# A two-block transformer kernel: the weight buffers' place in a 1 KB row of SBUF moves from 64 to 96 bytes past the activations'

## Chip, cores, metric

One core of one Trainium2 chip. The metric is the device time of one execution of the whole program, in microseconds (us).

## What is computed

Two blocks run one after the other on `x` of 256 tokens x 1024 features, in float32, each of depth 2:

```python
def first_block(x, mem, ...):
    mem_n = rms_norm(mem, mem_norm_g)
    for l in range(DEPTH):
        h = rms_norm(x, pre_mix_g[l])
        mix = parallel_mixer(h, ...)          # LRU, forgetting attention, retention, then @ w_out
        x = x + rms_norm(mix, post_mix_g[l])
        h = rms_norm(x, pre_cross_g[l])
        x = x + rms_norm(memory_cross_attention(h, mem_n, w_cq[l], w_ck[l], w_cv[l], w_co[l]), post_cross_g[l])
        h = rms_norm(x, pre_ffn_g[l])
        x = x + rms_norm(swiglu(h, w_gate[l], w_up[l], w_down[l]), post_ffn_g[l])
    return x

def second_block(x, ...):
    for l in range(DEPTH):
        x = x + 0.5 * swiglu_2(rms_norm_2(x, ffn1_norm[l]), ...)
        # mixer: NSA, stick-breaking and sliding-window attention of h @ w_in[l], gated and summed, then:
        x = x + merged @ w_out[l]
        x = x + 0.5 * swiglu_2(rms_norm_2(x, ffn2_norm[l]), ...)
    return x
```

There are six feed-forward parts (1024 -> 2 x 2816 -> 1024), one in each layer of the first block and two in each of the second. They and the projections are nearly all of the arithmetic.

## The kernel before, in words

**Layout.** Activations are feature-major: 8 tiles (`KT`) of 128 features on the partitions, 256 tokens (`S`) along the free dimension. So one feature tile of `x`, `xn_hi`, `y_hi` and the like is exactly 1,024 bytes of a partition, and it begins at a fixed place in every 1 KB row. The program counts these places from the start of a 32-byte aligned base: the norms' operands `xn_hi`, `xn_lo`, the feed-forward's `hid_hi`, `hid_lo`, the memory's `mem_hi`, `mem_lo`, the mixer's `merged_hi`, `merged_lo` and the attention's `y_hi`, `y_lo` all begin at place 0.

**Weights.** All weights come as one stream of 332 slots (`ORDER`), each 1024 x 256, in two halves of [128, 4 x 256] float32. SyncE loads half m into ring buffer `raw[m % 4]` as soon as `w_lo` of half m - 4 has been made (`sync_program`). ScalarE copies it, rounded, to `w_hi[m % 4]` (`split_hi`, L919). VectorE writes the rest, `raw - w_hi`, to `w_lo[m % 4]` (`split_lo`, L1455). One feature tile of a weight buffer is 256 columns, 1,024 bytes, as well; a product takes 128 of the columns as its stationary operand, so those begin at the buffer's place or 512 bytes further.

**Products.** `products` (L304) makes a float32 product of three fp32r matmuls into one PSUM bank: hi x hi, hi x lo and lo x hi:

```python
for j, (a, b) in enumerate([(lhs[0], rhs[0]), (lhs[0], rhs[1]), (lhs[1], rhs[0])]):
    m = T.matmul(out, a, b, start=first and j == 0, stop=True, skip_group_check=True)
```

Each has a weight load of 128 columns (a row of the engine PEld in the profile) and streams 256 columns. In `slot_T` the weights are stationary and the activations stream; a slot is 2 halves x 2 column tiles x 4 feature tiles x 3 = 48 matmuls. In `slot_rows` it is the other way round: 128 tokens of `xn` or `mem` are stationary and the weights stream (in the trace, `bank<-w_hi,xn_hi`). A feed-forward part (`ffn`) is 11 gate slots and 11 up slots on `xn`, then 11 down slots on `hid`, 33 x 48 = 1,584 matmuls with hardly a wait between them. Between the parts `keep_busy` (L312) runs bf16 matmuls of 256 columns on `ones` while a norm is made.

**One place with other strides.** In the second block the compression of keys and values (`cmp_hidden_of`) keeps its activations in `y_hi` and `y_lo` as sixteen tiles of 30 columns, one behind the other, so 120 bytes apart, and takes them as stationary operands while the weights stream from the ring: `bank<-w_hi,y_hi 128*30`. Slot `k0` takes the first eight tiles, slot `k1` the last eight. Against the place where the weights' stream begins, the eight tiles of `k1` begin (modulo 1,024) at -128, -8, 112, 232, 352, 472, 592 and 712 bytes.

**Order.** Each engine's instructions are written out by hand, and semaphores join them. In the feed-forward part ScalarE and VectorE split one slot ahead of TensorE.

**The lines that are changed** stand in `build`, where SBUF is handed out in order of the calls:

```python
    x = sb("x", [P, KT, S])
    xn = sb("xn", [P, KT, S])
    xn_hi, xn_lo = sb("xn_hi", [P, KT, S], F32R), sb("xn_lo", [P, KT, S], F32R)
    y_hi, y_lo = sb("y_hi", [P, KT, S], F32R), sb("y_lo", [P, KT, S], F32R)

    sb("offset", [P, 16])
    raw = [sb(f"raw{r}", [P, HK, COLS]) for r in range(RING)]
```

`offset` is 64 bytes that nothing uses. All that is handed out behind it (`raw`, `w_hi`, `w_lo`, `sq`, `con` and the smaller tensors) lies 64 bytes further in the row than it would without it. `hid`, `mem` and `merged` lie ahead of `x`, in a region of their own that begins at the base.

Of the kernel before, what the change touches and what calls it, by code (L numbers as in the profile page):

```python
# [15 lines left out]
P = 128  # L16
# [83 lines left out]
def build(nc, A):  # L100
# [4 lines left out]
    def sb(name, shape, dt=F32):  # L105
        return nc.alloc_sbuf_tensor(name, shape, dt)[tuple(slice(None) for _ in shape)]
# [20 lines left out]
    x = sb("x", [P, KT, S])  # L127
    xn = sb("xn", [P, KT, S])
    xn_hi, xn_lo = sb("xn_hi", [P, KT, S], F32R), sb("xn_lo", [P, KT, S], F32R)
    y_hi, y_lo = sb("y_hi", [P, KT, S], F32R), sb("y_lo", [P, KT, S], F32R)  # L130

    sb("offset", [P, 16])
    raw = [sb(f"raw{r}", [P, HK, COLS]) for r in range(RING)]
    w_hi = [sb(f"w_hi{r}", [P, HK, COLS], F32R) for r in range(RING)]
    w_lo = [sb(f"w_lo{r}", [P, HK, COLS], F32R) for r in range(RING)]
# [2205 lines left out]
def program(nc, arrays):  # L2341
    A = {n: nc.dram_tensor("in_" + n, a.shape, mybir.dt.from_np(a.dtype), kind="ExternalInput").ap()
         for n, a in arrays.items()}
    for n in ("x", "mem"):
        A[n] = A[n].rearrange("p (k s) -> p k s", k=KT)
    A["out"] = nc.dram_tensor("out", (P, KT, S), F32, kind="ExternalOutput").ap()
    A["skew"] = nc.dram_tensor("skew", (P * 12 * VEC,), F32, kind="Internal").ap()
    A["vec"] = nc.dram_tensor("vec", (12, VEC), F32, kind="Internal").ap()
    build(nc, A)
# [12 lines left out]
```

## Time and profile before

| what | us |
|---|---|
| median of 3 runs (lowest to highest) | 2198.8 (2196.2 to 2199.8) |
| the profiled execution's own time | 2195.4 |
| its span, first to last instruction | 2194.1 |
| TensorE busy | 2117.1 (96%) |
| VectorE busy | 1402.8 (64%) |
| ScalarE busy | 1124.8 (51%) |
| GpSimd busy | 72.8 (3%) |
| HBM traffic | 164 GB/s over the span |

The page gives busy times, 40 slices of the span, the DMA queues and the chain of waits that ended last. Matmuls are pipelined: a matmul's row shows how long it lasted, and several overlap, so the rate at which they follow each other is read from their starts, or from the time of a long unbroken piece of the chain divided by the number of matmuls in it.

### The profile page before, as it was taken

To read this page: it belongs to the slowest core of one execution; us is meant where nothing else is said; L and a number is where in the kernel's file an instruction comes from. 1 tells how busy PE (TensorE), PEld (TensorE's weight loads), DVE (VectorE), ACT (ScalarE), POOL (GpSimd) and SP (SyncE) were. 2 spreads that over 40 slices of the span, in tenths; PEclk is the share of its full clock that TensorE was granted. 3 is DMA by queue.
4 is the path that set the end of the run, shared out by engine and by line. 5 is a ranking of instruction groups with operands and counts; after the bars stand their busy time and mean duration, and the time that the engine had idled before them with its cause. 6 is when DMAs were issued, how large, how long until landed. Compare 5 with 4: busy or idle time off the path is not lost.

```text
span 2194.1 us, 40831 instructions
## 1 busy us (share of the span) xinstructions
PE 2117.1 (96%) x17446; PEld 2034.0 (93%) x17446; DVE 1402.8 (64%) x2152; ACT 1124.8 (51%) x1757; POOL 72.8 (3%) x80
## 2 busy tenths in 40 slices
PE   6999999999998999999999999999999999999999
PEld 6889899989888999999997889999999988889999
DVE  5677466565766666566667667666666676677664
ACT  4565444444754544454456556544444466555443
POOL 5100000000000000000000000000000000000000
PEclk9999999999999999999999999999999999999999
DMA  6444346636343456656555324566566553235664
GB/s 221 154 131 142 118 156 201 215 120 198 118 142 98 148 193 203 191 169 196 196 170 173 97 97 153 184 194 206 175 195 208 174 175 125 86 126 177 197 197 150
DMA packets 98485, 360.33 MB, mean 164 GB/s; under 512 B 11136, under 2 KB 11149, under 8 KB 97920
## 3 DMA queue, kind: packets, MB, share of 16 engines
q1 hardware_dynamic: 96192, 349.22, 48.8%
q0 software_dynamic: 1680, 5.35, 0.8%
q8 instruction: 137, 2.24, 0.4%
q10 hardware_dynamic: 432, 3.15, 0.4%
q14 instruction: 44, 0.36, 0.1%
HBM read 356.61 MB, written 3.43 MB: 164 GB/s over the span
## 4 chain that ended last, share of the span: by engine, by line
PE 79%; DVE 13%; ACT 6%; issue 2%; DMA 1%; ACTq 0%; DVEq 0%; SPq 0%
PE bank L304 70%; DVE w_lo L1455 4%; ACT w_hi L919 2%; PE bank L416 1%; DVE rinv L1854 1%; PE bank L330 1%; PE bank L421 1%; DVE xn_lo L1477 1%; DVE sq L1517 1%; DVE x L1521 1%; ACT logit L1330 1%; PE bank L771 1%; PE bank L417 1%; DVE sq L2041 1%; DMA raw<-in_stream 1%
## 5 line engine op out<-in xcount | busy, mean ns | idle before, releaser
L1455 DVE TENSOR_TENSOR w_lo<-raw,w_hi 128x1024 fp32r<-128x1024 f32 x664 | 794.4, 1233 | 380.9 <-ACT w_hi L919 380.4
L304 PE MATMUL bank<-xn_hi,w_hi 128*128 128x256 f32 x3168 | 892.7, 282 | 39.6 <-DVE xn_lo L1477 29.1
L304 PE MATMUL bank<-xn_lo,w_hi 128*128 128x256 f32 x3168 | 881.5, 278 | 0.0
L304 PE MATMUL bank<-xn_hi,w_lo 128*128 128x256 f32 x3168 | 881.4, 278 | 0.0
L919 ACT ACTIVATE w_hi<-raw 128x1024 fp32r<-128x1024 f32 x664 | 672.5, 1050 | 235.7 <-PE bank L304 219.3
L304 PEld LDWEIGHTS bank<-xn_hi,w_hi 128*128 128x128 f32 x3168 | 598.5, 189 | 52.5 <-issue 27.9
L304 PEld LDWEIGHTS bank<-xn_lo,w_hi 128*128 128x128 f32 x3168 | 597.0, 188 | 1.3 <-issue 1.0
L304 PEld LDWEIGHTS bank<-xn_hi,w_lo 128*128 128x128 f32 x3168 | 596.8, 188 | 0.0
L304 PE MATMUL bank<-hid_hi,w_hi 128*128 128x256 f32 x1056 | 292.8, 277 | 0.0
L304 PE MATMUL bank<-hid_hi,w_lo 128*128 128x256 f32 x1056 | 292.8, 277 | 0.0
L304 PE MATMUL bank<-hid_lo,w_hi 128*128 128x256 f32 x1056 | 292.7, 277 | 0.0
L304 PEld LDWEIGHTS bank<-hid_hi,w_hi 128*128 128x128 f32 x1056 | 199.1, 189 | 0.0
L304 PEld LDWEIGHTS bank<-hid_hi,w_lo 128*128 128x128 f32 x1056 | 198.3, 188 | 0.0
L304 PEld LDWEIGHTS bank<-hid_lo,w_hi 128*128 128x128 f32 x1056 | 198.3, 188 | 0.0
L980 ACT ACTIVATE hid_hi<-act_t 128x512 fp32r<-128x512 f32 x66 | 41.7, 632 | 188.8 <-DVE act_t L1535 188.8
L976 ACT ACTIVATE act_t<-act_t 128x512 f32<-128x512 f32 x66 | 41.8, 633 | 180.7 <-DVE act_t L1530 180.7
L304 PE MATMUL bank<-y_hi,w_hi 128*128 128x256 f32 x384 | 108.5, 282 | 3.5 <-DVE y_lo L1465 2.8
L304 PE MATMUL bank<-y_hi,w_lo 128*128 128x256 f32 x384 | 107.0, 279 | 0.0
L304 PE MATMUL bank<-y_lo,w_hi 128*128 128x256 f32 x384 | 107.0, 279 | 0.0
L1465 DVE TENSOR_TENSOR hid_lo<-act_t,hid_hi 128x512 fp32r<-128x512 f32 x66 | 45.7, 693 | 51.0 <-ACT hid_hi L980 51.0
L304 PEld LDWEIGHTS bank<-y_hi,w_hi 128*128 128x128 f32 x384 | 72.3, 188 | 5.7 <-DVE y_lo L1465 3.6
L1535 DVE TENSOR_TENSOR act_t<-act_t,bank 128x512 f32<-128x512 f32 x66 | 45.4, 688 | 46.4 <-PE bank L304 46.4
(373 smaller groups left out, 2706.6 us busy)
## 6 DMA issues: line engine op xcount, KB each, us to landing
raw<-in_stream SPq DMA_DIRECT2D x664, 512.0 KB, 4.2
skew<-vec POOLq DMA_DIRECT2D x12, 192.0 KB, 4.1
table<-skew POOLq DMA_DIRECT2D x1, 1408.0 KB, 7.3
con<-in_con ACTq DMA_DIRECT2D x1, 1029.0 KB, 15.3
x<-in_x ACTq DMA_DIRECT2D x1, 1024.0 KB, 7.0
xn<-in_mem ACTq DMA_DIRECT2D x1, 1024.0 KB, 11.9
out<-x SPq DMA_DIRECT2D x4, 256.0 KB, 3.4
logit<-in_small POOLq DMA_DIRECT2D x3, 288.5 KB, 3.2
```

The source lines that it names most:

```text
L304: m = T.matmul(out, a, b, start=first and j == 0, stop=True, skip_group_check=True)
L330: m = T.matmul(misc[0][:, 0, :], avg, sq[:, k, :], start=k == 0, stop=k == KT - 1, skip_group_check=True)
L416: T.matmul(out, v_of(0), pT[:, 0:S], start=first, stop=False, skip_group_check=True)
L417: return T.matmul(out[:, P:S], v_of(1), pT[:, S:S + P], start=False, stop=last, skip_group_check=True)
L421: m = T.transpose(dst[:, to * P:(to + 1) * P], src[:, frm:frm + P], c("ident"))
L771: T.matmul(out[:, LATE], q[:, P:S], k, start=True, stop=True)
L919: AC.activation(w_hi[m % RING], raw[m % RING], ACT.Copy).then_inc(*hi_done.next())
L976: AC.activation(act_t, act_t, ACT.Silu).then_inc(*silu_made.next())
L980: AC.activation(hid_hi[:, 2 * j:2 * j + 2, :], act_t, ACT.Copy).then_inc(*hid_hi_made.next())
L1455: V.tensor_tensor(w_lo[m % RING], raw[m % RING], w_hi[m % RING].bitcast(F32), ALU.subtract).then_inc(*lo_done.next())
L1465: V.tensor_tensor(lo, src, hi.bitcast(F32), ALU.subtract).then_inc(*to.next())
L1535: V.tensor_tensor(act_t, act_t, dense[1], ALU.mult).then_inc(*up_read.next())
```

## The change

Another unused tensor of 64 bytes goes in ahead of `y_hi`, and the one ahead of the rings shrinks from 64 to 32 bytes. So `y_hi` and `y_lo` begin at place 64, and `raw`, `w_hi`, `w_lo` and all that follows at place 96. The weights are now 96 bytes further in a row than `xn`, `hid`, `mem` and `merged`, and 32 further than `y`. In all 32 bytes more are used. The instructions of every engine, their order and their waits are the same as before; only addresses differ.

```diff
     x = sb("x", [P, KT, S])
     xn = sb("xn", [P, KT, S])
     xn_hi, xn_lo = sb("xn_hi", [P, KT, S], F32R), sb("xn_lo", [P, KT, S], F32R)
+    sb("offset_y", [P, 16])
     y_hi, y_lo = sb("y_hi", [P, KT, S], F32R), sb("y_lo", [P, KT, S], F32R)
 
-    sb("offset", [P, 16])
+    sb("offset", [P, 8])
     raw = [sb(f"raw{r}", [P, HK, COLS]) for r in range(RING)]
     w_hi = [sb(f"w_hi{r}", [P, HK, COLS], F32R) for r in range(RING)]
     w_lo = [sb(f"w_lo{r}", [P, HK, COLS], F32R) for r in range(RING)]
```

## Rows read from the trace of the kernel before

**Rows 1.** The page, busy time by engine, and granted TensorE clock in 40 slices.

```profile
PE 2117.1 (96%) x17446; PEld 2034.0 (93%) x17446; DVE 1402.8 (64%) x2152; ACT 1124.8 (51%) x1757; POOL 72.8 (3%) x80
...
PEclk9999999999999999999999999999999999999999
```

**Rows 2.** The page, the chain that ended last: shares of the span by engine and line.

```profile
PE 79%; DVE 13%; ACT 6%; issue 2%; DMA 1%; ACTq 0%; DVEq 0%; SPq 0%
PE bank L304 70%; DVE w_lo L1455 4%; ACT w_hi L919 2%; PE bank L416 1%; DVE rinv L1854 1%; PE bank L330 1%; PE bank L421 1%; DVE xn_lo L1477 1%; DVE sq L1517 1%; DVE x L1521 1%; ACT logit L1330 1%; PE bank L771 1%; PE bank L417 1%; DVE sq L2041 1%; DMA raw<-in_stream 1%
```

**Rows 3.** Groups by line and form, TensorE: count, busy us, mean ns, idle before.

```profile
L304 PE MATMUL bank<-xn_lo,w_hi 128*128 128x256 f32 x3168 | 881.5, 278 | 0.0
...
L304 PE MATMUL bank<-hid_lo,w_hi 128*128 128x256 f32 x1056 | 292.7, 277 | 0.0
...
L304 PE MATMUL bank<-y_lo,w_hi 128*128 128x256 f32 x384 | 107.0, 279 | 0.0
...
L304 PE MATMUL bank<-w_hi,xn_lo 128*128 128x256 f32 x160 | 46.1, 288 | 0.0
...
L304 PE MATMUL bank<-merged_lo,w_hi 128*128 128x256 f32 x128 | 36.0, 281 | 0.0
L304 PE MATMUL bank<-mem_lo,w_hi 128*128 128x256 f32 x128 | 35.8, 280 | 0.0
...
L304 PE MATMUL bank<-w_hi,mem_lo 128*128 128x256 f32 x128 | 35.7, 279 | 0.0
```

**Rows 4.** The chain in order of time, long pieces: start us, us, what.

```profile
294.06 175.53 PE bank L304 x1488
...
753.90 168.94 PE bank L304 x1488
946.83 174.38 PE bank L304 x1536
...
1393.48 174.37 PE bank L304 x1536
1574.66 174.37 PE bank L304 x1536
...
2021.37 168.94 PE bank L304 x1488
```

**Rows 5.** Groups of VectorE in two stretches, 294 to 464 and 754 to 923.

```profile
L1455 DVE TENSOR_TENSOR w_lo<-raw,w_hi 128x1024 fp32r<-128x1024 f32 x63 | 75.1, 1223 | 45.8 <-ACT w_hi L919 45.8
...
L1455 DVE TENSOR_TENSOR w_lo<-raw,w_hi 128x1024 fp32r<-128x1024 f32 x63 | 75.1, 1223 | 43.7 <-ACT w_hi L919 43.7
```

**Rows 6.** Timeline of TensorE, 469 to 476: start us, us, what (merged).

```profile
471.24 4.97 PE L312 MATMUL bank<-ones 128*128 128x256 bf16 x44
```

**Rows 7.** Timeline of TensorE, slot `k1`: 1st, 19th, 24th product, and what follows.

```profile
1162.27 0.28 PE L304 MATMUL bank<-w_hi,y_hi 128*30 128x256 f32 x1
...
1164.37 0.28 PE L304 MATMUL bank<-w_hi,y_hi 128*30 128x256 f32 x1
...
1164.93 0.28 PE L304 MATMUL bank<-w_hi,y_lo 128*30 128x256 f32 x1
1165.05 0.59 PE L656 MATMUL bank<-sq,con 128*128 128x512 f32 x1
```

**Rows 8.** The page's costliest groups, the weights' split on VectorE.

```profile
L1455 DVE TENSOR_TENSOR w_lo<-raw,w_hi 128x1024 fp32r<-128x1024 f32 x664 | 794.4, 1233 | 380.9 <-ACT w_hi L919 380.4
```

**Rows 9.** Waits: who for whom, us in total, times, longest us.

```profile
PE bank L304 <- DVE w_lo L1455: 15.6, 22, 1.7
ACT w_hi L919 <- DMA raw<-in_stream: 14.2, 10, 3.0
...
SPq L2167 <- DVE w_lo L1455: 1941.0, 660, 24.6
```

**Rows 10.** The page's DMA issues: KB each, median us from issue to landing.

```profile
raw<-in_stream SPq DMA_DIRECT2D x664, 512.0 KB, 4.2
```

## The prediction

> **What bounds the kernel now.** I read the page's busy times first. TensorE works in 96% of the span, at full clock in every slice [rows 1]. VectorE, the next, has 64%. Then the chain that ended last: 79% of it lies on TensorE, 70% on one line, L304, the fp32r products. 13% lies on VectorE: 4% is the split of the weights (L1455), and the rest is norms and attention [rows 2]. So the kernel is a stream of some 15,700 products of 256 columns (from the counts in [rows 3] and their equals), and its time is this count by the pace of one.
>
> The pace is what must be read next, since the change touches no instruction. A row of matmuls shows latency (277 to 281 ns), not pace, because they overlap. The pace is in the chain's long pieces, where time over count gives it [rows 4]. The kernel has six feed-forward blocks of 33 slots x 48 = 1,584 products. Five of them show 168.94 / 1488 = 113.5 ns (twice), and 174.38 / 1536 = 113.5 ns (three times). The first block shows 175.53 / 1488 = 118.0 ns. The tiles, lines and shapes are the same, and the clock is full in both. The reader is to see that **the stream has two paces**, 113.5 and 118.0 ns. It keeps the one that it starts with for up to 175 us, and the difference is (175.53 - 168.94) / 1488 = 4.43 ns per product.
>
> VectorE is not the cause: its weight split takes 1223 ns in the slow block and 1223 ns in a fast one [rows 5]. The bf16 matmuls of the same 256 columns, which keep TensorE busy between blocks, run at (4.97 - 0.28) / 43 = 109.1 ns [rows 6], so both paces lie above what the engine can do with this many columns.
>
> **How much runs at the slow pace** can be read from mean durations. The products on `merged` last 36.0 / 128 = 281.3 ns, those on `hid` 292.7 / 1056 = 277.2 ns. One `hid` block in six is slow, so the fast duration is 277.2 - (281.3 - 277.2) / 5 = 276.4 ns. On this scale `xn` (278.2) is 38% slow, `y` (278.6) 46%, `mem` 67% (279.7) where it streams and 51% (278.9) where the weights do [rows 3]. The products with `xn` stationary (288.1) I count as slow altogether, though waits lengthen them too. That makes 3,600 + 530 + 530 (hid) + 380 (merged) + 260 + 200 + 480, about 6,000 products, and 6,000 x 4.43 ns = 26.5 us spent on the slow pace. It is an upper figure, because a product behind a wait is long as well. I take 24 us.
>
> **The change, part by part.**
>
> *Instructions.* Each queue issues the same instructions in the same order on the same tiles; none is added or removed, and no wait. That is 0 us.
>
> *The distance between the two operands of a product.* Before, weights lie 64 bytes further in a 1 KB row than `xn`, `hid`, `mem`, `merged` and `y`. Now it is 96 bytes for all but `y`, and 32 for `y`. A product streams one operand's 1,024 bytes while the next one's 512 bytes (128 columns) are loaded. Does distance act on the pace? Two readings of the trace point in different ways. Against: the weights' distance is +64 or -64 by which operand streams, and 512 more for the second column tile, and `mem`, `xn` and `y` show no third pace: the pieces are at 113.5 or 118. For: the compression's products [rows 7] take stationary tiles of 30 columns, each 120 bytes further than the last, against a stream that always begins at the same place. The first six tiles (18 products) take (1164.37 - 1162.27) / 18 = 117 ns each. The last two come at (1164.93 - 1164.37) / 5 = 112 ns. They begin 592 and 712 bytes past the stream's own start. So somewhere in the row the slow pace cannot hold, and the place of the load does matter. A shift of 32 bytes is a quarter of one such step, and 96 is still far from 592. So I take no new pace, and the share of the slow one as it is: **0 us**. The bounds come from the same rows: all products at 113.5 is -24 us, all at 118.0 is 9,700 x 4.43 ns = +43 us.
>
> The Trainium skill ("SBUF — State Buffer", section "SBUF: two separate sides") says that only the port pair shared by VectorE and GpSimd causes contention, and that TensorE never waits on anyone there. It also gives cachelines of 16 bytes, of which 32 is a multiple. By that page the layout could cost or bring nothing, and the sum would be 0 us. This trace agrees that VectorE is out of it [rows 5], but two paces for the same products [rows 4] are something the page does not foresee.
>
> The Trainium skill ("TensorE: Matmul & The Clock Gate", "Back-to-back issue gap") gives N / 2.4 + 2.5 ns, which is 109.2 ns for 256 columns. The bf16 row agrees with 109.1 ns [rows 6]; the fp32r products, at 113.5, do not.
>
> *Splits, norms, attention.* `raw`, `w_hi` and `w_lo` move together, so the split reads and writes at the same distances as before. Its mean over stages of different neighbours moves from 1223 [rows 5] to 1233 ns [rows 8], 0.8%. Taken on the 4% of the chain that it holds (88 us) this is 0.7 us either way, and I take 0. `sq`, the constants and the score buffers move by 32 bytes too; the same 0.8% on the other 9% of VectorE's share is 1.6 us.
>
> *The weights' transfers.* 512 KB land 4.2 us after issue, and SyncE waits for VectorE to free a buffer in 660 of 664 cases, 1941 us in total [rows 9, 10]; TensorE waited 15.6 us for weights, ScalarE 14.2 us for a transfer. A landing slower by a few tenths of a microsecond at an odd 32 bytes would be covered by this slack: 0 us, and at most the doubling of the 14.2 us.
>
> The sum is 0 us. The profiled execution took 2195.4 us (span 2194.1), 3.4 under the median of 2198.8, and the runs shown span 3.6 us. I predict against the median: 2198.8 us. A measurement of this kernel can tell about 0.2%, 4.4 us, from no change.
>
> **The rivals.**
>
> 1. *The slow pace goes, or mostly does.* At 96 bytes the load may no longer meet what holds it. For it: near 592 bytes it does not hold, and 96 is a step in that direction (608 for the second column tile, already past it). Against: at 64 and 576 it holds. All gone gives 2175; only the first feed-forward block turned fast gives 1,584 x 4.43 = -7 us, 2192. Chance 0.34, partial cases included.
>
> 2. *More blocks start slow* (the other side). A block keeps the pace of its first products, so the start decides, and one slow start costs 7.0 us. The price is at the head of a feed-forward block, on TensorE; it decides from one further block on: 2206 for one, 2220 for three. For it: the first block shows that such a start happens, and the compression's tiles at 112 bytes and beyond are slow [rows 7], to which 96 is nearer than 64. Against: five of six start fast. Chance 0.16.
>
> 3. *The fast pace is lost altogether*: +43 us, 2242. For it: `merged` never has the fast one [rows 3]. Against: `hid` at the same distance has it. Chance 0.14.
>
> 4. *The pace falls to the bf16 one*, 109.1 ns: 9,700 x 4.4 + 6,000 x 8.9 = 96 us, 2103. Nothing in the rows shows an fp32r product stream there. Chance 0.03.
>
> 5. *The change does nothing*, because only whole rows or 64-byte pieces count, or since the paces come from timing alone. It gives my forecast, and is part of its chance.
>
> **How the numbers follow.** My forecast (shares of both paces within about 1,000 products of now, 2194 to 2203) has 0.33. Faster by over 0.2% has rivals 1 and 4: 0.37. Slower has rivals 2 and 3: 0.30. The range goes from 2172, all of rival 1 with 3 us of scatter, to 2225, rival 2 with three blocks and the scatter. It leaves out rivals 3 and 4, 0.17. The likeliest case's own range is 2194 to 2203.
>
> **What would show it.** Right: the chain's six long pieces again at 113.5 or 118.0 ns, one slow; `hid` near 277 ns; the split at 1233 ns; landing at 4.2 us. Rival 1: `hid`, `xn` and `merged` near 276 ns. Rivals 2 and 3: `hid` at 278 or more, 281 if all is lost. A third pace, in any long piece, would prove the step wrong in which the distance is given no new pace; a changed split or landing, those on the splits and the transfers.

## The result and the profile after

The changed kernel takes 2240.0 us (median of 4 runs, 2238.3 to 2244.6) against 2199.1 us (4 runs, 2196.2 to 2199.8): the ratio is 1.0172, with a 95% interval of 1.0129 to 1.0214. It is slower by 41 us, outside the range of 2172 to 2225. The profiled execution took 2238.3 us, span 2237.0.

The page's busy times, clock, and chain, as in [rows 1, 2]:

```profile
span 2237.0 us, 40831 instructions
...
PE 2166.3 (97%) x17446; PEld 2083.6 (93%) x17446; DVE 1403.0 (63%) x2152; ACT 1125.6 (50%) x1757; POOL 72.8 (3%) x80
...
PEclk9999999999999999999999999999999999999999
...
PE 82%; DVE 11%; ACT 5%; issue 1%; DMA 0%; DVEq 0%; ACTq 0%; SPq 0%
```

The counts are the same and the clock is full in every slice. TensorE is busy 49.2 us longer, VectorE 0.2 us and ScalarE 0.8 us. The loss is on TensorE alone. The chain's long pieces (start us, us, what), the six feed-forward blocks, answer to [rows 4]:

```profile
295.77 174.86 PE bank L305 x1488
...
757.33 174.86 PE bank L305 x1488
956.24 180.49 PE bank L305 x1536
...
1410.78 180.49 PE bank L305 x1536
1598.09 182.54 PE bank L305 x1536
...
2056.31 176.86 PE bank L305 x1488
```

Time over count gives 117.5 ns per product in four blocks and 118.9 or 118.8 ns in two (called 118.8 below). Counted from the start of one product to the start of the next, every level is about 0.2 ns lower (117.3 here, 113.3 and 117.8 before), since a piece's time also holds a little of its first and last product. **The pace of 113.5 ns is gone, and the levels are others**: before, a block ran at 113.5 or at 118.0. The six pieces hold the same 9,072 products as before and take 1070.1 us instead of 1036.5, which is 33.6 us of the 42.9 us by which the span grew. Outside the blocks the fast pace is gone too: no 25 products in a row with loads of 128 columns start less than 117.2 ns apart on average, where before the least was 113.3 ns.

The groups by line and form, against [rows 3]:

```profile
L305 PE MATMUL bank<-xn_lo,w_hi 128*128 128x256 f32 x3168 | 889.5, 281 | 0.0
L305 PE MATMUL bank<-hid_lo,w_hi 128*128 128x256 f32 x1056 | 295.9, 280 | 0.0
...
L305 PE MATMUL bank<-y_lo,w_hi 128*128 128x256 f32 x384 | 107.9, 281 | 0.0
L305 PE MATMUL bank<-w_hi,xn_lo 128*128 128x256 f32 x160 | 46.6, 291 | 0.0
...
L305 PE MATMUL bank<-merged_lo,w_hi 128*128 128x256 f32 x128 | 35.9, 280 | 0.0
```

`hid` went from 277.2 to 280.2 ns, `xn` from 278.2 to 280.8, `y` from 278.6 to 281.0. `merged`, all of whose products were slow in the profiled execution of before, lost nothing (281.3 to 280.5).

What the forecast held for unchanged is unchanged. The split on VectorE and the transfers, against [rows 8, 10]:

```profile
L1456 DVE TENSOR_TENSOR w_lo<-raw,w_hi 128x1024 fp32r<-128x1024 f32 x664 | 794.5, 1232 | 391.4 <-ACT w_hi L920 390.9
...
raw<-in_stream SPq DMA_DIRECT2D x664, 512.0 KB, 4.2
```

And the waits, against [rows 9], where TensorE's wait for weights fell by 4.1 us. A slower stream leaves the engines that feed it more time, which would explain it; no run tests that.

```profile
PE bank L305 <- DVE w_lo L1456: 11.5, 20, 1.5
```

### The profile page after: what moved, and what is told of

It reads as the page before. It is cut to its first block, busy times and chain, and to the rows that moved or that the text cites. A ratio compares the mean times of both kernels' runs of the same rounds, so it can differ in the third digit from the quotient of the medians.

```text
span 2237.0 us, 40831 instructions
## 1 busy us (share of the span) xinstructions
PE 2166.3 (97%) x17446; PEld 2083.6 (93%) x17446; DVE 1403.0 (63%) x2152; ACT 1125.6 (50%) x1757; POOL 72.8 (3%) x80
## 4 chain that ended last, share of the span: by engine, by line
PE 82%; DVE 11%; ACT 5%; issue 1%; DMA 0%; DVEq 0%; ACTq 0%; SPq 0%
PE bank L305 73%; DVE w_lo L1456 3%; PE bank L417 1%; ACT w_hi L920 1%; DVE rinv L1855 1%; PE bank L422 1%; PE bank L331 1%; PE bank L772 1%; DVE xn_lo L1478 1%; PE bank L418 1%; DVE sq L1518 1%; DVE x L1522 1%; DVE sq L2042 1%; DMA raw<-in_stream 0%; DVE scale L1496 0%
## 5 line engine op out<-in xcount | busy, mean ns | idle before, releaser
L1456 DVE TENSOR_TENSOR w_lo<-raw,w_hi 128x1024 fp32r<-128x1024 f32 x664 | 794.5, 1232 | 391.4 <-ACT w_hi L920 390.9
L1531 DVE TENSOR_TENSOR act_t<-bank,scale 128x512 f32<-128x512 f32 x66 | 45.6, 691 | 53.3 <-PE bank L305 53.1
```

The lines of the kernel that those rows point to most:

```text
L1456: V.tensor_tensor(w_lo[m % RING], raw[m % RING], w_hi[m % RING].bitcast(F32), ALU.subtract).then_inc(*lo_done.next())
L1531: V.tensor_tensor(act_t, dense[0], scale_2, ALU.mult).then_inc(*gate_read.next())
```

## The experiments

Every experiment is the kernel before with other places in the row. "Distance" is how far the rings lie past `xn`, `hid`, `mem` and `merged`, in bytes (`y` too, unless said). Where a diff shows only the line of `offset`, its width gives the distance: `[P, 16]` is 64.

### Is it the distance, the place, or something else that moved?

**128 bytes for all.**

```diff
-    sb("offset", [P, 16])
+    sb("offset", [P, 32])
```

> Weights 128 bytes further in the 1 KB row than all activations (64 before, 96 in the change). Theory A, the pace depends on the distance between the two operands modulo 64 bytes (0 allows 113.5 ns per product, 32 does not): 128 is 0 modulo 64, so about 2199 us, within 10 us, and feed-forward pieces of the chain at 113.5 or 118.0 ns. Theory B, it is the absolute place of the weights, off a 64-byte boundary: 128 is on one, so also about 2199 us. Theory C, the distance itself, the larger the worse: 2240 us or more, and no long piece at 113.5 ns.

Measured: 2250.1 us against 2199.2, ratio 1.0214 (1.0133 to 1.0296). The first feed-forward piece:

```profile
296.10 176.84 PE bank L304 x1488
```

That is 118.8 ns. Theory A falls, and theory B, since the rings are back on a multiple of 64 bytes from the base here, as before.

**Everything by 32 bytes, distance 64.**

```diff
+    sb("shift", [P, 8])
     base = (nc.sbuf_base + 31) // 32 * 32
```

> Every tensor of the kernel before moved by 32 bytes, activations and weights together, so the distance stays 64 and only the absolute places go off the 64-byte boundaries. Theory A (distance modulo 64): about 2199 us, within 10 us, long pieces at 113.5 or 118.0 ns. Theory B (absolute place of the weights): about 2240 us, long pieces at 117.3 to 120 ns as in the changed kernel. Theory C (size of the distance): about 2199 us.

Measured: 2201.6 us (8 runs) against 2199.2, ratio 1.0005 (0.9974 to 1.0036). Two blocks of the chain:

```profile
1585.78 174.37 PE bank L305 x1536
2032.87 168.95 PE bank L305 x1488
```

113.5 ns again, with every tensor 32 bytes off the places of before. So this shift of the absolute places costs nothing; what the two operands have between them does. Other common shifts were not run.

**Only what lies behind the rings, by 32 bytes.**

```diff
+    sb("offset_rest", [P, 8])
     sq = sb("sq", [P, KT, S])
```

> Rings and y stay where they were before; only what lies behind the rings (squares, constants, small operands, score buffers) moves by 32 bytes, as in the change. Theory D, the loss comes from norms and attention through these tensors: a good part of the 41 us, above 2215 us. Theories A, B and C: within 5 us of before, 2194 to 2204 us.

Measured: 2199.4 us (8 runs) against 2199.2, ratio 0.9997 (0.9958 to 1.0036). Theory D falls: norms, constants and score buffers have no part in it.

**Only `y`, by 32 bytes (distance 32 for `y`, 64 for the rest).**

```diff
+    sb("offset_y", [P, 8])
     y_hi, y_lo = sb("y_hi", [P, KT, S], F32R), sb("y_lo", [P, KT, S], F32R)
...
-    sb("offset", [P, 16])
+    sb("offset", [P, 8])
```

> Only y_hi and y_lo move, by 32 bytes; rings, constants and all else stay at their places of before, so the distance is 32 for the attention outputs' streams and 64 for the rest. Theory: the change's loss lies in each stream by its own distance. The y streams (1,152 products) go to 118.5 ns, at most 5 ns x 620 products that were at 113.5, so +3 us; xn and hid keep 113.5 or 118.0 ns, and the time is that of before on this chip within 8 us.

Measured: 2199.5 us (8 runs) against 2203.6 (21 runs), ratio 0.9987 (0.9957 to 1.0017). Groups by form:

```profile
L305 PE MATMUL bank<-xn_lo,w_hi 128*128 128x256 f32 x3168 | 880.1, 278 | 0.0
L305 PE MATMUL bank<-hid_lo,w_hi 128*128 128x256 f32 x1056 | 292.3, 277 | 0.0
...
L305 PE MATMUL bank<-y_lo,w_hi 128*128 128x256 f32 x384 | 107.9, 281 | 0.0
```

`y` has the 281 ns of the changed kernel, `xn` and `hid` keep the 278 and 277 of before. Each stream follows its own distance. The half of the change that moves `y` costs less than this measurement tells. By subtraction, the loss lies in the 96 bytes of the rest.

**TensorE's own reads, or the other engines?** When the rings move, so does all that ScalarE, VectorE and the transfers read and write in them. These accesses could slow the stream instead of TensorE's own. The kept traces can settle this. Every stretch of six products in a block was sorted by what another engine did in it: idle means busy for under 5% of the stretch, busy over 95%. The mean time from one start to the next, in ns, is:

| block | VectorE idle / busy | ScalarE idle / busy | no DMA packet in flight / some all the time |
|---|---|---|---|
| before, first (slow) | 117.77 / 117.79 | 117.78 / 117.78 | 117.80 / 117.78 |
| before, second (fast) | 113.31 / 113.35 | 113.35 / 113.33 | 113.36 / 113.33 |
| changed, first | 117.33 / 117.33 | 117.33 / 117.33 | 117.33 / 117.33 |

The levels are the same whatever the others do, so no access of theirs at that moment makes them. What is left is TensorE's load of one operand and its stream of the other.

### Which distances have the fast pace?

**32 bytes.**

```diff
-    sb("offset", [P, 16])
+    sb("offset", [P, 8])
```

> Weights only 32 bytes further than all activations, y included. Theory A (modulo 64) and theory B (absolute place): about 2240 us, all long pieces at 117.3 ns or above. Theory C (the larger the distance the worse): faster than 2199 us or the same, with long pieces at 113.5 ns.

Measured: 2249.8 us, ratio 1.0213 (1.0127 to 1.0299), and 118.5 ns in every block:

```profile
296.00 176.34 PE bank L304 x1488
```

Theory C falls with it: a smaller distance is as bad as a larger one.

**192 bytes** (`[P, 48]`).

> Weights 192 bytes further than all activations. So far 64 gave 2199 us, and 32, 96 and 128 gave 2240 to 2250. Theory E, the pace depends on the distance modulo 128 bytes and only near 64 can a stream run at 113.5 ns: 192 is 64 modulo 128, so about 2199 us within 12, with xn and hid pieces at 113.5 or 118.0 ns. Theory C (the further, the worse, past 64): 2240 us or more. Theory F, the period is longer than 128 (256, 512 or the whole row): 2240 us or more too.

Measured: 2240.0 us against 2214.1, ratio 1.0118 (1.0064 to 1.0171). Feed-forward blocks all ran at 118.0 ns, so the time that theory E gave, that of before within 12 us, did not come. But 113.5 ns exists here too. In this stream, in which the weights stream past stationary `xn`, the 44 products from the first row to the second take 4.99 us, 113.4 ns each (timeline of TensorE: start us, us, what):

```profile
82.85 0.28 PE L304 MATMUL bank<-w_hi,xn_hi 128*128 128x256 f32 x1
...
87.84 0.28 PE L304 MATMUL bank<-w_hi,xn_lo 128*128 128x256 f32 x1
```

So 192 has the levels of 64, and more of its streams start in the slow one.

**No offset** (the line of `offset` removed).

> No offset: weights and activations begin at the same place of a row. Theory E (modulo 128): 0 is the same as 128, so about 2250 us, with long pieces at 118.5 or 120 ns. If the period is longer than 128 the levels differ from those of 128 bytes: any other pace.

Measured: 2267.7 us, ratio 1.0242 (1.0213 to 1.0272), with 120.2 ns in every block:

```profile
298.60 178.81 PE bank L303 x1488
```

At 128 bytes five blocks had 118.8, the last 120.2. So 0 and 128 share one level, and whether they share both is not shown by one profiled execution of each.

**576, 448 and 320 bytes** (`[P, 144]`, `[P, 112]`, `[P, 80]`).

> Weights 576 bytes further: 64 plus 512, so the two column tiles of a weight buffer (512 bytes apart) change places, and the set of distances, 64 and 576 modulo the row, is the one of before. Theory H, only these distances modulo 512 count: pieces at 113.5 or 118.0 ns alone, time within 15 us of before on this chip. If the size of the distance counted: all at 117 ns or above, 40 us more.

> Weights 448 bytes further, which is 64 short of 512: the mirror of 64 if only distances modulo 512 count. The streams of before in which the weights stream and xn is stationary had this distance and showed 113.5 and 118.0 ns. Expected: the same two levels for all streams, the share of 113.5 open (192 had the levels too, but little of the fast one). If the sign counts: no piece at 113.5.

> Weights 320 bytes further, 64 modulo 128 and 256. If the levels repeat every 128 bytes: pieces at 113.5 or 118.0 ns only, as at 64 and at 192, time between before and 2245 us. If the period is longer: other levels, such as 118.5 or 120.

Measured against 2203.6 us: 2201.8 for 576 (ratio 1.0006, 0.9960 to 1.0052), 2233.2 for 448 (1.0162, 1.0082 to 1.0243), 2210.6 for 320 (1.0020, 0.9975 to 1.0064). One block at 118.0 ns and one at 113.5 from the chain of each, in this order:

```profile
1584.36 181.18 PE bank L304 x1536
2038.42 168.94 PE bank L304 x1488
```

```profile
1599.24 181.18 PE bank L304 x1536
2055.08 168.92 PE bank L304 x1488
```

```profile
752.14 175.52 PE bank L304 x1488
951.70 174.37 PE bank L304 x1536
```

The blocks of all three have the two levels of 64 and no other. So the fast level comes back at every distance tried that is 64 modulo 128, and at no other. In the one profiled execution of each, two of six blocks were fast at 576, one at 448 and four at 320.

**How many streams are fast sets the time.** In the profiled execution of each kernel that has the two levels, each unbroken run of 24 or more products with the same activations was counted as fast or slow by its mean pace (the line drawn at about 115 ns):

| kernel | slow products | us | us less 4.43 ns for each |
|---|---|---|---|
| before | 4,805 | 2195.4 | 2174.1 |
| only `y` moved | 4,745 | 2196.6 | 2175.5 |
| only the rest moved | 4,089 | 2198.9 | 2180.7 |
| all moved | 7,122 | 2206.9 | 2175.4 |
| 320 | 5,668 | 2208.4 | 2183.3 |
| 576 | 8,418 | 2212.5 | 2175.2 |
| 448 | 12,154 | 2229.1 | 2175.3 |
| 192 | 14,054 | 2235.1 | 2172.9 |

The times spread over 40 us. With the slow products taken off at the price of the prediction, six of the eight agree within 2.6 us, though they come from several chips; two have 5 to 10 us more, which stay unexplained. So 192 and 448 lose their time because few of their streams are fast, and not by another pace.

### How wide is the place around 64?

**80 and 48 bytes.** The rings are given places with `sb_at` inside one block, since `sb` rounds to 32 bytes; for 80:

```diff
-    sb("offset", [P, 16])
-    raw = [sb(f"raw{r}", [P, HK, COLS]) for r in range(RING)]
...
+    ring_at = (nc.sbuf_base + 31) // 32 * 32 + 64
+    sb("rings", [P, 12 * HK * COLS + 24])
+    ring = lambda name, dt, n: sb_at(name, [P, HK * COLS + 8], dt, ring_at + 4096 * n)[
+        :, 4:4 + HK * COLS].rearrange("p (k c) -> p k c", k=HK)
+    raw = [ring(f"raw{r}", F32, r) for r in range(RING)]
...
```

> Weights 80 bytes further, 16 past the place of before. It asks how wide the good place is. Theory E with a place some 32 bytes wide (as the compression's tiles of 30 columns suggest, of which 72 and 80 bytes modulo 128 ran at 113.5): 2175 to 2210 us, pieces at 113.5 ns. If only the exact 64 is good: 2235 us or more, no piece at 113.5 ns.

> Weights 48 bytes further, 16 short of the place of before. Theory E with a place centred on 64: like 80 bytes, 2175 to 2210 us. With a place that begins at 64 and lies above it: 2235 us or more, and 80 is the better of the two.

Measured against 2214.1 us: 2265.7 for 80 (ratio 1.0234, 1.0182 to 1.0285), 2242.2 for 48 (1.0128, 1.0085 to 1.0170). No block is at 113.5 in either: 80 has 119.0 ns in five and 118.8 in one, 48 has 118.0 in all. A fast place some 32 bytes wide, by which both were expected at 2175 to 2210 us, falls.

**56, 72, 60 and 68 bytes**, with the same lines and other numbers:

> Weights 56 bytes further, 8 short of 64. At 64 a stream can run at 113.5 ns or at 118.0 by its start; at 48 and 80 only at 117.5 or more. If the good place has a width of 8 bytes or more to this side: pieces at 113.5 ns, time at or below before. If the fast pace here holds from any start: all six long pieces at 113.5 ns and about 24 us less than before on this chip. If not: 118 ns throughout and 2235 us or more.

> Weights 72 bytes further, 8 past 64. Same question to the other side: with a width of 8 bytes pieces at 113.5 ns, and if any start leads there about 24 us less than before on this chip; without it 118 ns or more throughout and 2240 us or more.

> Weights 60 bytes further, one float32 element short of 64. With a good place at least one element wide to this side: both levels or the fast one alone, at most the time of before. If the place is exactly 64 modulo 128: no piece at 113.5 ns, 2235 us or more.

> Weights 68 bytes further, one element past 64. As for 60, to the other side: both levels or the fast one alone if the place is wider than one element, otherwise no piece at 113.5 ns and 2235 us or more.

Measured against 2202.4 us: 2242.8 for 56 (ratio 1.0192, 1.0116 to 1.0267), 2246.4 for 72 (1.0208, 1.0151 to 1.0265), 2261.4 for 60 (1.0276, 1.0217 to 1.0335), 2249.0 for 68 (1.0220, 1.0158 to 1.0281). The first block of 60 and of 68 in the chain:

```profile
297.47 178.06 PE bank L307 x1488
```

```profile
295.81 176.35 PE bank L307 x1488
```

119.7 and 118.5 ns. One float32 element to either side of 64 and the fast pace is gone from all six blocks.

Two things besides the distance set these six kernels apart. Their weights begin off a multiple of 32 bytes, which no kernel with the fast pace has, and their rings are handed out by `sb_at`, which was not run at 64 itself. The split on VectorE keeps its 1232 to 1234 ns and the transfers their 4.1 to 4.2 us in all six, but whether TensorE's fast pace needs the distance or an aligned place as well is not separated. What is shown is that, of the places tried, only those 64 bytes apart modulo 128, all multiples of 32, have it.

| distance | ns per product in the six blocks | time / before |
|---|---|---|
| 0 | 120.2 | 1.0242 |
| 32 | 118.5 | 1.0213 |
| 48 | 118.0 | 1.0128 |
| 56 | 118.0 | 1.0192 |
| 60 | 119.7 | 1.0276 |
| 64 | 113.5 or 118.0 | 1 |
| 68, 72 | 118.5 | 1.0220, 1.0208 |
| 80 | 118.8 or 119.0 | 1.0234 |
| 96 (the change) | 117.5 or 118.8 | 1.0172 |
| 128 | 118.8 or 120.2 | 1.0214 |
| 192 | 118.0 (113.5 in short streams) | 1.0118 |
| 320, 448, 576 | 113.5 or 118.0 | 1.0020, 1.0162, 1.0006 |

The ratios come from several chips, each measured against its own runs of the kernel before. They rest on two runs of each changed place, but on four for 96 and eight for 320 and 576. None of these places beats 64 by more than its interval.

## Why the prediction was wrong

**The reading was right.** TensorE's stream bounds the kernel, its time is count by pace, and the pace has levels that a block keeps from its start. The instructions, the split (1233 to 1232 ns), the transfers (4.2 us before and after) and the rest behind the rings (ratio 0.9997 by itself) cost nothing, as each was priced. Two readings were a little off. I took some 6,000 slow products and 24 us; the count, in runs of 24 or more, is 4,805 and 21 us. And the compression's last two tiles do not run at 112 ns: from the 19th product to what follows the 24th, (1165.05 - 1164.37) / 6 is 113.3 ns [rows 7], which is the fast pace and no other.

**The step that failed** is the one on the distance: "So I take no new pace, and the share of the slow one as it is: 0 us." In its place stands: at 96 and at 32 bytes no block and no long stream ran at 113.5 ns, and the blocks have 117.5, 118.5 or 118.8 ns. The argument against an effect was that distances of +64, -64 and 512 more all show the same two paces. That holds, and it was read the wrong way. All of these are 64 modulo 128, the one class that has the fast pace, so they could not show what another class does. The trace of before had no product of `products` with loads of 128 columns outside that class.

**The bound was right where the choice was not.** Rival 3, the fast pace lost altogether, gave 2242 us; 2240.0 was measured. I gave it a chance of 0.14 and left it out of the range. Its price was 9,700 products by 4.43 ns, from 113.5 to 118.0. That it fits so well is in part luck, since the blocks have lost the level of 118.0 ns as well; they happen to average 1070.1 us / 9,072 = 118.0 ns. Measured by blocks, the five that were fast lost 4.0 or 5.3 ns a product (113.5 to 117.5 or 118.8), and the first, which had been slow, won 0.45 ns (118.0 to 117.5). The argument against it, that `hid` keeps the fast pace at the same distance as `merged`, spoke of 64 bytes and not of 96.

**The compression's tiles misled.** I took from their last two [rows 7] that the fast place lies near 592 and 712 bytes and is some width apart from 64. In the changed kernel the good tiles of the same slot are others (1st, 10th, 19th and 24th product):

```profile
1177.93 0.28 PE L305 MATMUL bank<-w_hi,y_hi 128*30 128x256 f32 x1
...
1178.98 0.28 PE L305 MATMUL bank<-w_hi,y_hi 128*30 128x256 f32 x1
...
1180.01 0.28 PE L305 MATMUL bank<-w_hi,y_hi 128*30 128x256 f32 x1
...
1180.60 0.28 PE L305 MATMUL bank<-w_hi,y_lo 128*30 128x256 f32 x1
```

The first nine products take 117 ns each (1.05 / 9), the next nine 114 (1.03 / 9), the last five 118 (0.59 / 5). The fast tiles moved from the seventh and eighth to the fourth to sixth. So they do depend on places, which was the point for an effect, but loads of 30 columns follow a rule that the 128-column streams do not share: 592 and 712 are 80 and 72 modulo 128, and at these distances the feed-forward blocks ran at 119.0 and 118.5 ns. So the width of the good place there (two or three tiles) said nothing of the blocks. That rule stays open.

**The margin of "no change" was too small.** I gave 0.2% from three runs within 3.6 us. Of the kernel before's 21 runs on one chip, 20 took 2189.7 to 2218.6 us, 1.3%, and one took 2225.5. Slow starts at 7 us a block are enough for this: the traces of kernels at distance 64 show other blocks slow each time, and the table of slow products ties their number to the time. Of the kernel before only one execution was profiled, so for its own scatter this is an inference.

The page of the Trainium skill that was weighed ("SBUF — State Buffer", "SBUF: two separate sides") gave 0 us by the rule that TensorE never waits on anyone at its ports. No run here contradicts the rule for other engines, since VectorE's split took 1223 ns in a fast and in a slow block [rows 5] and the pace did not change with VectorE, ScalarE or the transfers busy. But the pace does change with where TensorE's two operands lie to each other: the measured levels from 113.5 to 120.2 ns decide against the reading that the layout can cost TensorE nothing.

## What stays open

Why the distance of 64 modulo 128 has a fast pace at all, and what at a stream's start decides between 113.5 and 118.0 ns, no run tells. Nor is it known why 192 and 448 draw the fast one less often than 64, 320 and 576, whether the other levels repeat with 128 bytes too, or whether a common shift of both operands by less than 32 bytes keeps the fast pace.

## What to carry to other kernels

Where fp32r products of 256 columns follow each other with a weight load each, and all tiles have a pitch of 1 KB, try the two operands' buffers 64 bytes apart, both on multiples of 32 bytes. It was worth 1.7% here over 96 bytes and 2.4% over none, for 64 bytes of memory. 320 and 576 bytes did as well; 192 and 448, though also 64 modulo 128, took 1.2% and 1.6% longer. One kernel shows this, and no other was tried. Read the pace from a long piece of the chain, time over count, and not from the mean duration or the busy share. When several cases in a trace agree that a quantity does not matter, first ask whether they differ in the respect that the change will alter.

## What the runs showed of the hardware

- The pace of fp32r products (128 x 128 loads, 256 columns) is between 113.5 and 120.2 ns at full clock by the places of the two operands in a partition alone; as far as one common shift by 32 bytes shows, it is their distance that counts. The bf16 matmuls of the same width kept 109.1 ns: (4.97 - 0.28) / 43 before [rows 6], and (6.06 - 0.28) / 53 in the timeline of the changed kernel:

```profile
472.28 6.06 PE L313 MATMUL bank<-ones 128*128 128x256 bf16 x54
```

- The levels do not change when both operands move together by 32 bytes (ratio 1.0005), nor with VectorE, ScalarE or the transfers idle or busy (117.3 ns in each case in the changed kernel's first block).
- One element (4 bytes) off the good distance costs as much as 32 bytes or more: 119.7 and 118.5 ns at 60 and 68 bytes, 118.5 at 32.
- A stream keeps its level for 1,536 products, up to 184.6 us (with no offset), without a change.
- Which of its two levels a stream gets is worth 4.43 ns a product, and in eight profiled executions the number of slow products (4,089 to 14,054) accounts for most of the spread from 2195.4 to 2235.1 us.
